# Merging the branches of a two-layer hybrid model: weights, branches and sum split into high and low parts, three products for each block

## The reference, cut to what matters

```python
def hybrid_mixer(h, w_in, ..., w_up_dn, w_up_sb, w_out):      # layers 0 and 1
    ...
    y_dn = o.reshape(B, S, DN_V).astype(h.dtype) @ w_up_dn          # 1024 x 1024
    ...
    y_sb = o_sb.reshape(B, S, SB_W).astype(h.dtype) @ w_up_sb       # 512 x 1024
    g_dn, g_sb = jnp.split(jax.nn.sigmoid(gates), N_BRANCH, axis=-1)
    return (g_dn * y_dn + g_sb * y_sb) @ w_out                      # 1024 x 1024

def second_block(x, ...):                                     # the third block
    ...
        merged = (gates[:, :, 0] * (y_ssd @ w_ssd_br[layer]).astype(F32)      # 1024 x 1024
                  + gates[:, :, 1] * (y_dil @ w_dil_br[layer]).astype(F32)    #  256 x 1024
                  + gates[:, :, 2] * (y_mem @ w_mem_br[layer]).astype(F32))   #  768 x 1024
        h = h + merged.astype(h.dtype) @ w_out[layer]                         # 1024 x 1024
```

## Time and profile before

| | us |
|---|---|
| median of 3 runs | 3945.53 |
| lowest and highest run | 3940.39, 3948.24 |
| the profiled execution's own time | 3948.66 |
| its span, from first to last instruction | 3946.8 |
| PE busy with matmuls | 3571.6 |
| DVE busy | 2435.3 |
| ACT busy | 1824.6 |

### The profile page before, as it was taken

The page is one execution under the profiler, slowest core; times in us unless marked ns, Lnnn a source line. Parts: engine busy times, 40 slices in busy tenths (PEclk is TensorE's granted clock), DMA queues, the critical chain, the costliest instruction groups (busy, mean ns, idle before and its releaser), DMA issues. The chain is left out here.

```text
span 3946.8 us, 54104 instructions
## 1 busy us (share of the span) xinstructions
PE 3571.6 (90%) x21361; PEld 3119.6 (79%) x21361; DVE 2435.3 (62%) x3003; ACT 1824.6 (46%) x1988; POOL 56.0 (1%) x36
## 2 busy tenths in 40 slices
PE   4988889989798799999999996898588899999999
PEld 4978779989687487777887775796367899977887
DVE  5847246468451388888888853544423688586665
ACT  3534234344330376676676642443222444464554
POOL 0000000000000000000000000000000000000000
PEclk6999989999999799999999998899789899999999
DMA  6730236458011299999999953352013455503554
GB/s 219 258 121 6 107 129 239 166 188 303 5 65 43 107 354 360 363 361 361 368 360 361 363 215 134 112 181 87 7 54 107 149 181 181 181 33 116 193 191 160
DMA packets 296867, 739.02 MB, mean 187 GB/s; under 512 B 17450, under 2 KB 17905, under 8 KB 291313
## 3 DMA queue, kind: packets, MB, share of 16 engines
q1 hardware_dynamic: 296688, 736.60, 52.3%
HBM read 735.50 MB, written 1.05 MB: 187 GB/s over the span
## 5 line engine op out<-in xcount | busy, mean ns | idle before, releaser
L1930 DVE TENSOR_TENSOR weight_ring_low<-weight_ring,weights_high 128x2048 fp32r<-128x2048 f32 x336 | 773.4, 2343 | 149.5 <-ACT weights_high L1876 149.5
L1876 ACT ACTIVATE weights_high<-weight_ring 128x2048 fp32r<-128x2048 f32 x336 | 618.3, 1907 | 8.1 <-DMA weight_ring<-in_moe_w 8.1
L374 PE MATMUL psum_all<-h_high_projections,high_projections 128*128 128x256 f32 x1536 | 440.6, 287 | 25.5 <-DVE h_low_projections L309 25.4
L374 PE MATMUL psum_all<-h_low_projections,high_projections 128*128 128x256 f32 x1536 | 436.8, 284 | 0.0
L374 PE MATMUL psum_all<-h_high_projections,weight_ring_low 128*128 128x256 f32 x1536 | 433.3, 282 | 0.0
L1818 PE MATMUL psum_all<-weights_high,expert_in_turn_high 128*128 128x512 f32 x896 | 360.0, 402 | 17.7 <-DVE weight_ring_low L1930 11.6
L1818 PE MATMUL psum_all<-weights_high,expert_in_turn_low 128*128 128x512 f32 x896 | 357.0, 398 | 0.0
L1818 PE MATMUL psum_all<-weight_ring_low,expert_in_turn_high 128*128 128x512 f32 x896 | 352.2, 393 | 0.0
L374 PEld LDWEIGHTS psum_all<-h_high_projections,high_projections 128*128 128x128 f32 x1536 | 293.1, 191 | 30.1 <-DVE h_low_projections L309 30.1
L374 PEld LDWEIGHTS psum_all<-h_high_projections,weight_ring_low 128*128 128x128 f32 x1536 | 296.4, 193 | 0.0
L2791 PE MATMUL psum_all<-peer_h_high,expert_rows_high 128*128 128x256 f32 x1024 | 291.4, 285 | 5.0 <-DVE expert_rows_low L2839 5.0
(11 more groups left out here) (590 smaller groups left out, 7413.5 us busy)
## 6 DMA issues: line engine op xcount, KB each, us to landing
weight_ring<-in_moe_w SPq DMA_DIRECT2D x336, 1024.0 KB, 5.1
weight_ring<-in_w_in SPq DMA_DIRECT2D x48, 2048.0 KB, 8.6
expert_rows<-in_peer_down SPq DMA_DIRECT2D x128, 512.0 KB, 3.2
expert_rows<-in_peer_up SPq DMA_DIRECT2D x128, 512.0 KB, 3.2
weight_ring<-in_ffn_halves SPq DMA_DIRECT2D x42, 1024.0 KB, 6.0
branch_out<-in_ada_w SPq DMA_DIRECT2D x64, 512.0 KB, 9.7
weight_ring<-in_w_out SPq DMA_DIRECT2D x6, 2048.0 KB, 8.0
weight_ring<-in_ada_w SPq DMA_DIRECT2D x4, 2048.0 KB, 11.6
```

What stands on the lines that cost most here:

```text
L374: mm = pe.matmul(half(k.ps, 4 * (g % R) + j), w[:, c, j * P:(j + 1) * P], x[:, c], start=(c == 0 and n == 0), stop=(c == KC - 1 and n == 2))
L1876: act.activation(high[:, q, h * HALF:(h + 1) * HALF], k.ring[:, q, h * HALF:(h + 1) * HALF], ACT.Copy).then_inc(high_made[q], 1)
L1930: dve.tensor_tensor(k.low[:, q, part], k.ring[:, q, part], high[:, q, part].bitcast(F32), ALU.subtract).then_inc(low_made[q], 1)
```

## The change

`branches` gets the same scheme as `project`. ACT copies each source branch into a rounded high part (`source`), and each panel, in two halves, into `weights_high` (`split`), which has `H = 2` places. DVE subtracts, which gives the low part of the source in place and that of the panel in the ring slot (`low`). PE makes three float32r products for each block (`three`). The last branch is merged in two halves of four blocks, ACT and DVE split the sum in the same halves, and the output product waits for `merged_split`. The loop on DVE places the `low` of later panels ahead of `branch(i)`, up to panel `p + 1`, with p the panels of the parts up to i. `high` lies over the first 32 blocks of `projected`, `merged_high` over `tmp`, `merged_low` over `merged`. Calls pass the sources' addresses along. SP's order and waits are the same as before.

```diff
-    n_all = sum(len(p) for p, _ in parts) + 2
...
+    H = 2
+    HALF = SLOT // 2
     first = parts[0][0][0][0]
+    panels = [(g, kb) for group, _ in parts for g, kb in group] + [(wout, None), (wout + 1, None)]
+    n_all = len(panels)
...
+        source_high = k.sb(f"source_high_{name}", [P, n_src, T], F32R, ctx=ctx)
+        high = alias("weights_high", k.proj_at, [P, H, SLOT])
+        merged_high, merged_low = alias("merged_high", tmp_at, [P, KC, T]), alias("merged_low", merged_at, [P, KC, T])
+        source_low = [alias(f"source_low{i}", x_at, [P, x.shape[1], T]) for i, (_, (x, x_at)) in enumerate(parts)]
...
             @block.scalar
             def _(act):
+                def source(i):
+                    x = parts[i][1]
+                    act.activation(source_high[:, at[i]:at[i] + x.shape[1]], x, ACT.Copy).then_inc(source_made, 1)
+
+                def split(p, n):
+                    g = panels[p][0]
+                    act.wait_ge(k.loaded[g % R], k.value[g])
+                    if p >= H:
+                        act.wait_ge(k.used, g - H + 1)
+                    act.activation(high[:, p % H, part(p, n)], k.ring[:, g % R, part(p, n)], ACT.Copy).then_inc(high_made, 1)
+                source(0)
+                split(0, 0)
+                split(0, 1)
+                for i in range(1, len(parts)):
+                    source(i)
+                split(1, 0)
+                split(1, 1)
                 for i in range(len(parts)):
                     act.activation(gate_of(i), gate_of(i), ACT.Sigmoid).then_inc(opened, 1)
-
...
+                for p in range(2, n_all):
+                    split(p, 0)
+                    split(p, 1)
+                for n in range(2):
+                    act.wait_ge(taken, len(parts) + n)
+                    act.activation(merged_high[:, 4 * n:4 * n + 4], merged[:, 4 * n:4 * n + 4], ACT.Copy).then_inc(merged_made, 1)
 
...
-                for i, (panels, src) in enumerate(parts):
+                def three(out, p, c, cols, kb, hi, lo, start, stop):
+                    g = panels[p][0]
+                    w_hi = high[:, p % H, 0:2 * width(p)].rearrange("p (c n) -> p c n", c=kb)[:, c, cols]
+                    w_lo = k.low[:, g % R, 0:2 * width(p)].rearrange("p (c n) -> p c n", c=kb)[:, c, cols]
+                    for n, (w, x) in enumerate(((w_hi, hi), (w_hi, lo), (w_lo, hi))):
+                        mm = pe.matmul(out, w, x, start=start and n == 0, stop=stop and n == 2)
+                    return mm
...
+                    pe.wait_ge(source_split, i + 1)
+                    src_hi = source_high[:, at[i]:at[i] + x.shape[1]]
+                    src_lo = source_low[i]
+                    if group[0][1]:
+                        pe.wait_ge(low_made, 2 * (p + len(group)))
...
+                        for m in range(len(group)):
                             for j in range(4):
                                 for c in range(KC):
-                                    mm = pe.matmul(place(i, 4 * m + j), w[:, c, j * P:(j + 1) * P], src[:, c],
-                                                   start=(c == 0), stop=(c == KC - 1))
+                                    if j == 0 and c % 4 == 0:
+                                        pe.wait_ge(low_made, 2 * p + c // 4 + 1)
+                                    mm = three(place(i, 4 * m + j), p, c, slice(j * P, (j + 1) * P), KC, src_hi[:, c], src_lo[:, c],
+                                               c == 0, c == KC - 1)
                             mm.then_inc(k.used, 1)
...
                 pe.wait_ge(taken, len(parts))
                 for m in range(2):
-                    g = wout + m
-                    pe.wait_ge(k.loaded[g % R], k.value[g])
...
+                            if j == 0 and c % 4 == 0:
+                                pe.wait_ge(low_made, 2 * p + c // 4 + 1)
+                                if m == 0:
+                                    pe.wait_ge(merged_split, c // 4 + 1)
+                            mm = three(place(len(parts), 4 * m + j), p, c, slice(j * P, (j + 1) * P), KC, merged_high[:, c], merged_low[:, c],
...
                     mm.then_inc(k.used, 1)
...
-                n_used = first
-                for i, (panels, _) in enumerate(parts):
-                    n_used += len(panels)
...
+                def source(i):
+                    x = parts[i][1]
+                    dve.wait_ge(source_made, i + 1)
+                    dve.tensor_tensor(source_low[i][:], x, source_high[:, at[i]:at[i] + x.shape[1]].bitcast(F32), ALU.subtract).then_inc(source_split, 1)
+
+                def low(p, n):
+                    g = panels[p][0]
+                    dve.wait_ge(high_made, 2 * p + n + 1)
+                    dve.tensor_tensor(k.low[:, g % R, part(p, n)], k.ring[:, g % R, part(p, n)], high[:, p % H, part(p, n)].bitcast(F32),
+                                      ALU.subtract).then_inc(low_made, 1)
+
+                def branch(i, n_used):
                     dve.wait_ge(k.used, n_used)
                     dve.wait_ge(opened, i + 1)
-                    ps = place_rows(k.ps, P)[:, 8 * (i % 2):8 * (i % 2) + 8]
-                    if i == 0:
-                        dve.tensor_tensor(merged[:], ps, gate_of(i), ALU.mult).then_inc(taken, 1)
-                    else:
-                        dve.wait_ge(taken, i)
-                        link(dve.tensor_tensor(tmp[:], ps, gate_of(i), ALU.mult))
-                        dve.tensor_tensor(merged[:], merged[:], tmp[:], ALU.add).then_inc(taken, 1)
+                    last = i == len(parts) - 1
...
+                        blocks = slice(0, 8) if n is None else slice(4 * n, 4 * n + 4)
...
+                        if i == 0:
+                            dve.tensor_tensor(merged[:, blocks], ps, gate_of(i)[:, blocks], ALU.mult).then_inc(taken, 1)
+                        else:
+                            dve.wait_ge(taken, i)
+                            link(dve.tensor_tensor(tmp[:, blocks], ps, gate_of(i)[:, blocks], ALU.mult))
+                            dve.tensor_tensor(merged[:, blocks], merged[:, blocks], tmp[:, blocks], ALU.add).then_inc(taken, 1)
+                source(0)
+                low(0, 0)
+                low(0, 1)
+                for i in range(1, len(parts)):
+                    source(i)
+                n_low, n_used, p = 1, first, 0
+                for i, (group, _) in enumerate(parts):
+                    p += len(group)
+                    n_used += len(group)
+                    while n_low < min(p + 2, n_all):
+                        low(n_low, 0)
+                        low(n_low, 1)
+                        n_low += 1
+                    branch(i, n_used)
+                for n in range(2):
+                    dve.wait_ge(merged_made, n + 1)
+                    dve.tensor_tensor(merged_low[:, 4 * n:4 * n + 4], merged[:, 4 * n:4 * n + 4], merged_high[:, 4 * n:4 * n + 4].bitcast(F32),
+                                      ALU.subtract).then_inc(merged_split, 1)
+                while n_low < n_all:
+                    low(n_low, 0)
+                    low(n_low, 1)
+                    n_low += 1
...
-                branches(k, f"branches{l}", [([(s[f"up_dn{l}"], None), (s[f"up_dn{l}"] + 1, None)], k.o[:, 0:8]),
-                                             ([(s[f"up_sb{l}"], 4)], k.proj[:, SQ0:SQ0 + 4])], (GD0, GS0), s[f"out{l}"], k.mod[:, l, 16:24],
+                branches(k, f"branches{l}", [([(s[f"up_dn{l}"], None), (s[f"up_dn{l}"] + 1, None)], (k.o[:, 0:8], k.o_at)),
+                                             ([(s[f"up_sb{l}"], 4)], (k.proj[:, SQ0:SQ0 + 4], k.proj_at + SQ0 * 4 * T))], (GD0, GS0), s[f"out{l}"], k.mod[:, l, 16:24],
```

More of the change, by code:

```diff
@@ L151, in __init__, with next_at @@
         self.issued = 0
+    def next_at(self):
+        return -(-self.nc.sbuf_base // 32) * 32
     def sb(self, name, shape, dt=F32, ctx=None):
@@ L1366, in gate_of, with place, width, part @@
                 return k.proj[:, gates[i]:gates[i] + 8]
+            def place(i, j):
+                return half(k.ps, 8 * (i % 2) + j)
+            def width(p):
+                kb = panels[p][1]
+                return HALF if kb is None else kb * D // 2
+            def part(p, n):
+                return slice(n * width(p), (n + 1) * width(p))
             @block.scalar
             def _(act):
+                def source(i):
[14 more added lines that the diff above has]
+                split(1, 1)
@@ L1379, in _ @@
+                p = 0
+                for i, (group, x) in enumerate(parts):
                     if i >= 2:
                         pe.wait_ge(taken, i - 1)
[L1381 to L1385, removed]
-                                pe.wait_ge(k.loaded[g % R], k.value[g])
-                        else:
-                            pe.wait_ge(k.loaded[panels[0][0] % R], k.value[panels[0][0]])
+                    pe.wait_ge(source_split, i + 1)
[3 more added lines that the diff above has]
```

(17 more changed lines are left out.)

31 lines of the change are left out of this document (21 added, 10 removed).

## The result

| | before | after |
|---|---|---|
| median of 5 runs, us | 3945.53 | 3964.90 |
| lowest and highest | 3940.01, 3955.58 | 3961.65, 3969.66 |
| profiled execution, its span | 3948.66, 3946.8 | 3961.65, 3959.9 |

The ratio is 1.005, with a 95% interval from 1.0031 to 1.0068: the changed kernel is slower by 12 to 27 us, 19.4 by the medians. The forecast was 3964.

What follows compares the result with a forecast made beforehand. PE's products set the pace, with one stop a call at the merge. Products -41.1 us, against dearer starts, merge waits and a second stop, gave +18.6 us on 3945.5: 3964, range 3953 to 3976.

Steps and rivals of the forecast that it cites:

- The products: PE's panels in the three calls: three float32r products take 11.31 us a panel instead of 13.88, together -41.1 us.
- The rule of four passes: Rival: plain float32 costs four equal passes, each new product one; 10.41 us a panel, +4.2 us in all, 3950; chance 0.05.
- The start: Start of each call: PE's first product waits for splits of the source and first half panel, +6.5 us each.
- The wait at the merge: PE's wait for the merged sum grows from 4.7 us: +8.0 in each of two calls, +16.3 in the third.
- The second stop: Third call, between branches 1 and 2: PE waits 6.1 us for panel 4's load and split; +7.9 with 1.8 for clock.
- The clock: Lower PE clock after a stop: 1.8 us added for the third call's new stop; elsewhere both kernels pay it.
- my sum: Terms over the three calls: +1.65 us in the first and second each, +15.3 in the third, together +18.6.
- the rival of the low clock: Rival: clock stays low for longer at all seven PE starts in the changed calls, +17 us, 3981; chance 0.08.

Runs made afterwards that it cites:

- halved source: Changed kernel with four edits: sum ahead of output panels not due, three places and narrow branch last in third call, first source split in halves; 3932.62 us, ratio 0.9964.
- order experiment: Changed kernel with the sum put ahead of the last output panel on ACT and DVE (both output panels on DVE in the third call); 3944.79 us, ratio 0.9999.
- third place: Changed kernel with three places for the high parts of panels instead of two, order as it is; 3960.63 us, ratio 1.0042 to before.
- delayed load: Changed kernel with one more 2048 KB load issued on SP right ahead of the third call's last output panel load; 3971.13 us, ratio 1.0067 to before.
- products in the wait: Changed kernel with unused PE products in the merge waits, 95 in the first two calls and 160 in the third; 3959.56 us, ratio 1.0033 to before.

## Why the prediction was right

**The products.** Forecast -41.1 us for 16 panels, from 13.88 to 11.31 us a panel. The residual groups stand 11.37 us apart in the calls shown, and PE's own rows 11.31. The rule of four passes (the Trainium skill, FP8 and Floating Point Precision, TensorE Precision Notes), if each of the new products cost one such pass, would have given 10.41. A quarter of a plain block's 0.434 us is 0.108, and one float32r product takes 0.118, so three products cost more than three of four such quarters. The measurement decides: this rival is out.

**The start.** Forecast +6.5 us a call. ACT's first row is at 441.00 and PE's first product of that call at 447.58, 6.6 us later. The halved source took 1.3 us off PE's wait, from 11.6 to 10.3.

**The wait at the merge.** Forecast 12.7, 12.7 and 21.0 us; measured 12.6, 12.6 and 20.5. The order experiment, the third place and the delayed load each moved it as the chain says, within 0.6 us of what was expected.

**The second stop.** Forecast 6.1 us; measured 5.8, from 2943.9 to 2949.7, with the load at its head.

**The clock** is the term that was mis-sized. I gave the new stop 1.8 us and the other starts no difference. The last branch loses 2.6 us instead, and the output products lose 2.1, 3.1 and 3.1 us where each lost 1.8. Behind the start of the second call PE loses 1.6 us, where it was 2.6, so not every start got dearer. Against the full pace (11.31 and 13.88 us a panel) PE loses 16.7 us behind the seven starts of the changed calls and 11.8 behind the six of before: +4.9, where the sum has +1.8. The waits came out 0.7 us shorter than forecast. Together this is the 2.4 us by which the calls (+21.0) exceed my sum (+18.6). It is the rival of the low clock in small: it gave 17 us more, and there are 3. That PE's idleness brings it was shown by the products in the wait; what makes one start dearer than another wasn't found.

**The whole.** 3964 against 3964.9. Some of that closeness is luck: the same kernel repeated was 22.2 us over before, a median here moves by 3 us, and in both traces the calls are 21.0 us longer and not 18.6.

## What to carry to other kernels

When work is made cheaper on the engine that sets the pace, look at what the new operands put ahead of its first product and into its waits; here 41 us were saved on PE, 57 given back in waits on two engines that had idle time and on a load, and 5 in PE's lower pace behind the waits. In an in-order queue, work that isn't due yet must stand behind the work that another engine waits for, above all if it waits for a slot or a load itself: that order alone was worth 20 us. A panel whose slot comes free only at the end of a group is loaded only then, here at 2969.32 us, when PE was already waiting for it; a narrow branch behind a wide one gives such loads time, though it was tried here only together with other edits.

## What the runs showed of the hardware that I had not expected

The price of an idle PE isn't fixed, and it doesn't go by the length of the wait: the same 192 products took 2.1 us longer than at the full clock after one wait of 12.6 us and 3.1 after another, 3.1 after 20.5 and 2.2 after 26.0; after 4.7 us the plain ones took 1.8 longer. Products that nobody uses bought it back (granted clock 1.00 instead of 0.92 in the output product of the first call), and with more work on PE the calls became 6.3 us shorter, the medians 5 to 9.
